# A two-block model on one core: attention's second branch in reversed row-block order, an earlier PSUM copy, and GpSimd's weight split with waits between its pieces

## What is computed

```python
for l in range(DEPTH):                       # DEPTH = 2
    h = rmsnorm(x, attn_norm[l])
    (q, kc, vc, ksl, vsl, kwn, vwn, gts, gq, gk, gv, ga, gr, uv) = split_columns(h @ w_in[l])
    o_nsa = nsa_mixer(...)                   # 8 heads: compressed, selected and window attention, gated
    o_gla = gla_mixer(...)                   # gated linear attention with decay
    o_sg = spatial_gating(uv, ...)
    x = x + concat([o_nsa, o_gla, o_sg]) @ w_out[l]
    h = rmsnorm(x, ffn_norm[l])
    x = x + (silu(h @ w_gate[l]) * (h @ w_up[l])) @ w_down[l]
```

## Time and profile before

| what | us |
|---|---|
| median of 3 runs | 2050.62 (2049.79 to 2055.84) |
| the profiled execution, its own time | 2054.61 |
| its span from first to last instruction | 2052.6 |
| TensorE busy | 1924.2 (94%), mean granted clock 0.969 |
| GpSimd busy | 1419.6 (69%) |
| VectorE busy | 1160.2 (57%) |
| ScalarE busy | 615.6 (30%) |

### The profile page before, as it was taken

How to read it: one execution, slowest core, us unless ns; L and a number is a source line. 1 busy time by engine, 2 the same in 40 slices (tenths; PEclk the granted TensorE clock), 3 DMA queues, 4 the chain that set the end, 5 groups by cost and what they waited for, 6 DMA issues and landing times.

```text
span 2052.6 us, 28491 instructions
## 1 busy us (share of the span) xinstructions
PE 1924.2 (94%) x10022; PEld 1489.2 (73%) x10022; DVE 1160.2 (57%) x1670; ACT 615.6 (30%) x1116; POOL 1419.6 (69%) x1208
## 2 busy tenths in 40 slices
PE   7898889999999999988899999997999999989997
PEld 5676557888888877755588888885777777768775
DVE  5765774466257347478556704654937666650353
ACT  4124662210011131266531100113036566540111
POOL 8554117988789985511298978886897878757772
PEclk9999989999999999999999999998999999999998
DMA  5132002343334222300124433542132233222221
GB/s 204 53 96 80 22 11 83 122 143 108 97 121 136 92 72 81 116 21 22 32 93 123 133 100 96 148 124 67 51 108 84 79 94 87 76 72 93 84 91 41
DMA packets 68680, 182.44 MB, mean 89 GB/s; under 512 B 23888, under 2 KB 24144, under 8 KB 68432
## 3 DMA queue, kind: packets, MB, share of 16 engines
q1 hardware_dynamic: 60480, 154.48, 24.8%
q10 hardware_dynamic: 8080, 26.32, 4.1%
HBM read 178.67 MB, written 2.10 MB: 88 GB/s over the span
## 4 chain that ended last, share of the span: by engine, by line
PE 70%; DVE 13%; ACT 7%; issue 6%; POOL 2%; DMA 1%; ACTq 0%; DVEq 0%; POOLq 0%
PE PS L402 21%; PE PS L406 20%; PE PS L405 20%; POOL w_lo L2083 2%; PE PS L691 1%; PE PS L653 1%; PE PS L641 1%; PE PS L441 1%; ACT P L1251 1%; ACT rg L1322 1%; DVE gN L1472 1%; DVE P L1946 1%; PE PS L538 1%; POOL w_hi L2079 1%; DVE PS L1620 1%
## 5 line engine op out<-in xcount | busy, mean ns | idle before, releaser
L2079 POOL TENSOR_TENSOR w_hi<-raw,const 128x256 fp32r<-128x256 f32 (+1 forms) x602 | 641.9, 1088 | 586.1 <-PE PS L402 578.2
L2083 POOL TENSOR_TENSOR w_lo<-raw,w_hi 128x256 fp32r<-128x256 f32 (+1 forms) x602 | 783.9, 1324 | 13.4
L402 PE MATMUL PS<-a_hi,w_hi 128*128 128x512 f32 x1616 | 651.7, 403 | 42.3 <-POOL w_lo L2083 14.1
L405 PE MATMUL PS<-a_lo,w_hi 128*128 128x512 f32 x1616 | 635.8, 393 | 0.0
L406 PE MATMUL PS<-a_hi,w_lo 128*128 128x512 f32 x1616 | 635.3, 393 | 0.0
L402 PEld LDWEIGHTS PS<-a_hi,w_hi 128*128 128x128 f32 x1616 | 307.1, 190 | 128.6 <-issue 46.0
L406 PEld LDWEIGHTS PS<-a_hi,w_lo 128*128 128x128 f32 x1616 | 307.2, 190 | 65.9
L405 PEld LDWEIGHTS PS<-a_lo,w_hi 128*128 128x128 f32 x1616 | 307.6, 190 | 64.8 <-issue 3.4
L1793 DVE TENSOR_TENSOR work<-PS,rstd 128x512 f32<-128x512 f32 x88 | 60.8, 691 | 147.6 <-PE PS L406 140.9
L402 PE MATMUL PS<-f_hi,w_hi 128*128 128x512 f32 x352 | 138.7, 394 | 0.0
L406 PE MATMUL PS<-f_hi,w_lo 128*128 128x512 f32 x352 | 138.0, 392 | 0.0
(11 more groups left out here) (290 smaller groups left out, 2494.1 us busy)
## 6 DMA issues: line engine op xcount, KB each, us to landing
raw<-weights SPq DMA_DIRECT2D x278, 512.0 KB, 3.5
work<-mod_w ACTq DMA_DIRECT2D x24, 512.0 KB, 3.6
work<-cmp_w ACTq DMA_DIRECT2D x8, 1024.0 KB, 5.6
bias<-rpb SPq DMA_DIRECT2D x256, 12.0 KB
rgw<-rgw ACTq DMA_DIRECT2D x8, 256.0 KB, 2.6
out<-xc SPq DMA_DIRECT2D x8, 256.0 KB, 2.0
const<-const SPq DMA_DIRECT2D x1, 1436.5 KB, 15.3
x<-x_t SPq DMA_DIRECT2D x4, 256.0 KB, 6.8
```

Source lines behind the costliest of these rows:

```text
L402: ins = nc.tensor.matmul(out, wh, hi, start=start, stop=False)
L405: nc.tensor.matmul(out, wh, lo, start=False, stop=False)
L2079: G.tensor_tensor(w_hi[:, r, k, :], raw[:, r, k, :], ones[:, k, :], ALU.mult).then_inc(pool_chain, 1)
L2083: ins = G.tensor_tensor(w_lo[:, r, k, :], raw[:, r, k, :], w_hi[:, r, k, :].bitcast(F32), ALU.subtract)
```

## The change

1. `row_block(u)` gives the row block of a unit. For even units (first branch) it is as before; for odd ones (second branch) it is reversed. A pair's widths in blocks go from 1, 1, 2, 2, 3, 3, 4, 4 to 1, 4, 2, 3, 3, 2, 4, 1.
2. ScalarE's copy of bank 6 stands right behind `exps(u + 2)`, ahead of `compressed_exps` and of the activations.
3. `rowok` is applied by ScalarE, as the scale of a 128x8 copy behind the sigmoid, and no more by VectorE.
4. The bank rotation starts at 0 in each layer.
5. GpSimd's split: the high part is a tensor-scalar multiplication by 1.0 (one input) in two pieces of 512; each is followed by its low part, in two pieces of 256 (most input slots, `fine_slot`) or one of 512 (the others), and GpSimd waits for each piece before the next within a slot. The loops are unrolled.

```diff
+def row_block(u):
+    i = u // 2 % NT
+    return i if u % 2 == 0 else NT - 1 - i
...
-                pool_of["banks"] = 4
+                pool_of["banks"], pool_of["next"] = 4, 0
...
-                    return u // (2 * NT), u // 2 % NT, u % 2
+                    return u // (2 * NT), row_block(u), u % 2
...
-                                                   start=False, stop=br == 1 and i == NT - 1 and n == i)
+                                                   start=False, stop=u % (2 * NT) == 2 * NT - 1 and n == i)
...
                         A(gN[:, :, :], PS[:, uses[(l, name, "T")][0], 0:NT * 24].rearrange("p (n c) -> p n c", c=24), ACT.Sigmoid)\
+                            .then_inc(act_chain.sem, 1)
+                        act.wait_ge(act_chain.sem, act_chain.raised())
+                        if l == 0:
+                            act.wait_ge(const_in, 16)
+                        A(gN[:, 0, 2:24:3], gN[:, 0, 2:24:3], ACT.Copy, scale=c_("rowok"))\
                             .then_inc(emptied((l, name, "T")), 1)
...
                     if u + 2 < U:
                         exps(u + 2)
+                    if u % 8 == 0 and u:
+                        t = u // 8 - 1
+                        act.wait_ge(*filling((l, "O", t)))
+                        A(proj[:, t, :], PS[:, 6, :], ACT.Copy).then_inc(emptied((l, "O", t)), 1)
+                        act.wait_ge(*emptying((l, "O", t)))
                     if u % (2 * NT) == 0 and u + 2 * NT < U:
                         compressed_exps(u // (2 * NT) + 1)
...
-                        g = gN[:, 0, 2:24:3]
-                        TS(g, g, c_("rowok"), None, ALU.mult).then_inc(dve_chain.sem, 1)
-                        dve.wait_ge(dve_chain.sem, dve_chain.raised())
...
+            def split(n, hi_parts, lo_parts):
+                r = n % RING
+                pool.wait_ge(raw_in[r], 16 * (n // RING + 1))
+                if n >= RING:
+                    pool.wait_ge(slot_used, n - RING + 1)
+                each, per = 8 // hi_parts, lo_parts // hi_parts
+                for h in range(hi_parts):
+                    k = slice(h * each, (h + 1) * each)
+                    G.tensor_scalar(w_hi[:, r, k, :], raw[:, r, k, :], 1.0, None, ALU.mult).then_inc(pool_chain, 1)
+                    spent[0] += 1
+                    pool.wait_ge(pool_chain, spent[0])
+                    for q in range(h * per, (h + 1) * per):
+                        k = slice(q * 8 // lo_parts, (q + 1) * 8 // lo_parts)
+                        ins = G.tensor_tensor(w_lo[:, r, k, :], raw[:, r, k, :], w_hi[:, r, k, :].bitcast(F32), ALU.subtract)
+                        if q < lo_parts - 1:
+                            ins.then_inc(pool_chain, 1)
+                            spent[0] += 1
+                            pool.wait_ge(pool_chain, spent[0])
+                ins.then_inc(split_done, 1)
...
+                return item[0] == "in" or item[0] == "out" and item[2] < 2 or item[0] == "in2" and item[1] < 6 * KT
```

More of the change, by code:

```diff
@@ L1120, in exps @@
                 def exps(u):
-                    i, br = u // 2 % NT, u % 2
+                    i, br = row_block(u), u % 2
                     w = (i + 1) * P
@@ L1139, in _ @@
                 for u in range(U):
-                    i, par = u % NT, u % 2
-                    w = (u // 2 % NT + 1) * P
+                    par = u % 2
+                    w = (row_block(u) + 1) * P
                     if u >= 2:
@@ L1172, in _ @@
                             act.wait_ge(to_dve.sem, to_dve.raised())
[L1173 to L1178, removed]
                     if CONVERT_FROM <= u < U - 1:
@@ L1658, in scale @@
                 def scale(u):
-                    j, i, br = u // (2 * NT), u // 2 % NT, u % 2
+                    j, i, br = u // (2 * NT), row_block(u), u % 2
                     w = (i + 1) * P
@@ L2067, in _ @@
             G = nc.gpsimd
[L2069 to L2083, removed]
+            spent = [0]
@@ L2084, in split, with fine_slot @@
                 ins.then_inc(split_done, 1)
-            def pieces_of(turn):
-                return PIECES if any(beside_vector(item) for item in PLAN[turn * RING:(turn + 1) * RING]) else 1
+            def fine_slot(n):
+                item = PLAN[n]
+                return item[0] == "in" or item[0] == "out" and item[2] < 2 or item[0] == "in2" and item[1] < 6 * KT
             pool.wait_ge(head_in, 16)
[L2091 to L2103, removed]
-                else:
[L2105 to L2109, removed]
@@ L2112, in _ @@
+            for n in range(SLOTS):
+                if n and fine_slot(n):
+                    split(n, 2, 4)
+                else:
+                    split(n, 2, 2)
         @block.sync
```

## The result

The change makes the kernel slower: 2074.18 us (median of 4 runs, 2069.77 to 2074.38) against 2052.77 us (2049.79 to 2055.84), ratio 1.0099 with a 95% interval of 1.0076 to 1.0122. The forecast was 2018.5, with 2003 to 2036 as its range. It is rival A, to which the prediction gave 0.07. The profiled execution has a span of 2071.4 us (2052.6 before) at a mean granted clock of 0.979 (0.969 before).

A forecast was written before the change was run, and what follows sets the result against it. TensorE, 94% of the span and full in the feed-forward stretch, was taken as the bound, so only its waits pay. Gains 7.7 + 11.8 + 4.8 + 0 + 8 = 32.3 us against 2050.62 gave 2018.5 us, range 2003 to 2036.

The forecast's parts named there:

- rival A: Coarse GpSimd slots: one-input form is slow, TensorE waits in each of 170 slots beyond 1.19 us a piece; 2132 at 1.5; chance 0.07.
- GpSimd (part 5): GpSimd's split: high pieces of 0.8 us, shorter VectorE waits in operations with two SBUF inputs; gain 8 us, bounds -3 and 17.
- coarse slot: GpSimd slot of two high pieces and two low ones of 512, with pauses: 4.7 us, under TensorE's 5.44.
- pauses: GpSimd's gap behind each piece: costs 0.08 us, should let VectorE's waiting operations in.
- rowok (part 3): First layer's decay chain, L441 to its group of eight: chain starts 12 us earlier; gain 11.8 us, bounds 8 to 12.5.
- Rival B: First layer's decay chain: pauses do not let VectorE in, 128x4 operations wait instead; 11.8 and half of 8 go, 2034; chance 0.09.
- Bank rotation (part 4): Second layer, product behind the sum over squares: no wait for bank 0's eviction; gain 7.7 us, bounds 5.1 to 7.8.
- Early copy (part 2): Attention, units 16 and 8: TensorE waits less for ScalarE's copy of bank 6; gain 4.8 us, bounds 1 and 9.
- Reversed order (part 1): Attention of both layers: same total work in either order, costed at nothing, with -6 to +8 us.
- y_lo: VectorE's eight y_lo of L2038: mean from 1.555 to near 1.1 us; half of 17 us of TensorE loss there taken, 8.

The follow-up runs named there:

- e1: The changed kernel with two-input high pieces (times a tile of ones) instead of one-input ones, pauses kept; 2036.99 us, ratio 0.9916 to the kernel before.
- f2: The changed kernel with two-input high pieces and no pauses, both high pieces ahead of the low ones; 2029.12 us, ratio 0.9882 to the kernel before.
- f3: The changed kernel with its one-input high pieces but no pauses, both high pieces ahead of the low ones; 2034.04 us, ratio 0.9905 to the kernel before.
- e6: The kernel before with only rowok moved from VectorE to ScalarE; 2056.84 us, ratio 1.0018.
- e4: The kernel before with only the change's GpSimd split (one-input high parts of 512, pauses, written out); 2086.6 us, ratio 1.0146.
- g4: f2 with high parts in four two-input pieces of 256 in the fine slots, still written out; 2027.51 us, ratio 0.9868 to the kernel before.
- e3: The changed kernel with GpSimd's old split (pieces of 1024 or four of 256, a loop); 2039.33 us, ratio 0.9928 to the kernel before.

## Why the prediction was wrong, point by point

- **GpSimd (part 5)** is the step that failed: the duration T of the one-input high piece. Between an upper end of 1.16 us and a lower one of 0.63 I took 0.8, "because one operand less is read". It measures 1.49 undisturbed, 1.58 on average, above the upper end. That end was itself a safe reading of the two-input piece (1.04 undisturbed, 1.14 in e1), and was wrong as an upper end for another form: a row of ScalarE and a row of another operation bound nothing on GpSimd. I took 4.7 us for the coarse slot, under the 5.44 in which TensorE uses it up; it is 5.78, and TensorE waits. The Trainium skill (GPSIMD Engine Reference, Engine selection) calls one-input work on GpSimd roughly line rate; these rows contradict it, and the measurement decides.
- The **price** followed rival A's mechanism and not its size. Its threshold, T = 1.19, was passed, and its formula gives (2 x 1.49 + 3.06 - 5.44) x 170 = 102 us (the changed kernel has 185 such slots, by its 370 low pieces of 512). Measured are 51.1: the low piece is 0.12 us shorter than taken, so the undisturbed slot is 5.78 and not 6.04, and the loss falls in the 53 + 52 slots that start late, at 5.95 and 5.92 us each: 53 x 0.51 + 52 x 0.48 = 52 us. Each stretch has some 73 slots; in the first 20 of each GpSimd's lead covers the difference, and in the coarse slots elsewhere TensorE leaves it time.
- I treated the **pauses** as a small cost (0.08 us each, which is right) with a likely gain. The cost matters only in a slot that is full already, and there it was 34 us. With two-input pieces the gain did not exist (f2). With one-input pieces VectorE's waits are shorter with the pauses (busy 1008.7 us, 1054.0 in f3), and no gain in time shows from it.
- **rowok (part 3)**: a gain of 11.8 us came in the stretch that I named, but not by this edit (e6: nothing; e4: all of it without the edit). I had seen that the wait lasts until GpSimd has nothing to do, and yet costed the edit as if the wait belonged to the operation. Rival B had this right: what is waited out is GpSimd's run, and another operation takes its place. In this chain VectorE got in without the pauses (f2, f3), and did not with high pieces of 256 (g4).
- **Bank rotation (part 4)**: 7.7 us forecast, 7.7 measured, wherever GpSimd kept its pace; 6.2 in the changed kernel, whose two slots there were GpSimd's.
- **Early copy (part 2)**: 4.8 forecast, 3.9 measured in attention (total 0.9982 of before). **Reversed order (part 1)**: nothing forecast, nothing measurable.
- **y_lo**: its mean fell from 1.56 to 1.18 us with the change (median 1.30 to 0.98), near the 1.1 forecast, and the last stretch gained 8.7 us, where half of some 17 was taken. The number is right in part by luck, since the mean is not what pays: in e1 and f2 it is still 1.50 and the stretch gained 8.4. What fell there too is the longest one, from 2.77 to 1.67 us, and in f2 TensorE's waits in the stretch for VectorE's `y_lo`, `a_lo` and `tmp` of L2031, from 7.3 to 3.1 us; in the changed kernel they are gone. (The wait of 2.5 us for the sum stays in all.)

## What to carry to other kernels

Price an instruction form only by rows of that engine and that form; where the trace has none and the engine's slack per unit is a few tenths of a us over a hundred units, the unknown form is the main risk and not a 0.07. A wait for a shared resource belongs to the run that holds it: moving the waiting operation away only picks the next one. And a slower instruction can still pay if the engine has slack where it runs and its neighbour works freely beside it: choose the form by place.

## What the runs showed that was not expected

- On GpSimd a one-input tensor-scalar over 128x512 takes 1.49 us, and a two-input tensor-tensor, one of its inputs a column read over and over, 1.04 (medians over 556 pieces each).
- VectorE's busy sum is lower beside the one-input form, though f3 has the long waits above: its busy time for the same work is 1160.2 us before, 1079.6 in f2, 1054.0 in f3, 1093.2 in e1 and 1008.7 in the changed kernel.
- A run of GpSimd's two-input pieces of 256 without a gap kept one operation of VectorE out for 16.55, 14.92, 14.86 and 6.55 us (before, e6, e3, g4). With high pieces of 512 in the run (f2) it got in behind the next piece; in f3 fourteen waited over 2 us, some of them past two low pieces of 512. The Trainium skill (SBUF — State Buffer, Who interferes with whom) has the loser wait for the other's instruction to end; f2 agrees, the runs of 256 and f3 do not.
